# Two blocks on one core: the rows between the blocks are transposed from the sums, with both norms' gains joined in the column factor

## The chip, the cores and the metric

The kernel runs on one core of a Trainium2 chip. The metric is the device time of one execution in microseconds, the median of the runs shown. The engines are called as the profile calls them: PE (TensorE), ACT (ScalarE), DVE (VectorE), POOL (GpSimd) and SP, whose queue issues the weight loads.

## What is computed

The input is 256 rows of 1024 columns. A first block of two layers and a second block of two layers follow each other. Between them stand two norms in a row, one at the end of the first block and one at the start of the second:

```python
def rms_norm(x, g):
    xf = x.astype(jnp.float32)
    y = xf * lax.rsqrt(jnp.mean(xf * xf, axis=-1, keepdims=True) + EPS)
    return (y * g.astype(jnp.float32)).astype(x.dtype)

# first block, its end
    h2 = rms_norm(x, norm2_g[l])
    x = x + jnp.square(jax.nn.relu(h2 @ w_up[l])) @ w_down[l]
    return rms_norm(x, final_norm_g)
# second block, its start
    h = x
    xn = rmsnorm(h, norm_mix[0])
    h = h + hybrid_mixer(xn, w_in[0], ...)
```

So the normed rows of the first block are both the residual stream `h` of the second block and the input of its first norm. With `r1` the root of the sums' rows and `r2` that of the second norm, the first product of the second block reads `x * final_norm_g * norm_mix` per column, times `r1 * r2` per row.

## The kernel before

All weights are streamed through the core in pieces of 512 rows by 512 columns (1 MB). SP loads a piece; ACT casts it to a high part `WH` in two halves (L1608); DVE subtracts that from the piece and gets the low part `WL`, in two halves too (L2169); PE multiplies high by high, low by high and high by low (L744, L745, L746, or L730, L731, L736 where the activations have just been turned). There are three places for cut pieces, so a piece is cut two pieces ahead of its use, and its cut waits until PE is done with the piece three before.

The activations lie transposed in `XTH` and `XTL`. `half` makes one half of them, 512 columns of both row tiles, in two steps: PE transposes four blocks into a bank (L841), ACT writes the high part with the norm's gain as factor per column (L1619, L1620), DVE the low part (L2181). The norm's factor per row (`rs`) is left out here and comes in when a product is read out of PSUM.

Each engine's program is written by hand, and each engine takes its instructions in that order. A generator per engine walks the same list of pieces; small tasks are put in a list `side` and advance one step at each `tick`.

The place of the change is the seam between the blocks. The last down projection of the first block (`mlp1`, layer 1) adds its sums to the rows `X` in two column halves (`add_x`, L2347). The second block then starts with the product `vf` (260 columns, pieces of 4 blocks), then `qkb` (512 columns), and so on.

- DVE, `first_of_two` (L2452): waits for the gain `GB1`, spread over the partitions by a load at L560, multiplies the first column half of both row tiles by it into `XN` (`times_gain(0)`, L2449, 2 instructions), and makes the low part of half 0.
- PE transposes `XN`; its half 0 waits for `tg.at(0)` (L1071), half 1 for `tg.at(1)` (L1475).
- DVE, `two_norms` (L2456), called at the first step of `vf`: `times_gain(1)`, the low part of half 1, then the numbers of the norms. The second mean is taken of `XN` and scaled by `r1` twice (L2462, L2464); POOL makes both roots (L629, L630, each L610 and L612); DVE joins them to `rs` (L2466) and writes the normed rows back, `X = XN * r1` (L2468, 2 instructions).
- ACT, `two_norms` (L1840): the high part of half 1, then per row tile the squares of `X` and the squares of `XN` (L1844, L1845), and one signal `n2q` at the end.
- The first reader of `rs` is ACT's read-out of `vf` (L1869). The forget gate follows as a side task, `fox_gate`: DVE L2552 to L2559, a power on POOL (L633), a logarithm on ACT (L1873), DVE L2565, and then two small sums over rows on PE (L1092 to L1094), which stand in PE's order behind the first row tile of the second `qkb` piece.

Of the kernel before, what the change touches and what calls it, by code (L numbers as in the profile page):

```python
# [12 lines left out]
ALU = mybir.AluOpType  # L13
ACT = mybir.ActivationFunctionType
# [225 lines left out]
def program(nc, dr, cf, cb, ci, out):  # L240
    ctx = ExitStack()
    with ctx:
# [139 lines left out]
        for l in range(2):  # L382
            for key, ap, n in ((("n1", l), dr["norm1_g"], 8), (("n2", l), dr["norm2_g"], 8), (("nm", l), dr["norm_mix_2"], 8),
# [3 lines left out]
                if key != ("n1", 0):  # L387
                    k = sum(v[1] for v in rows.values())
                    rows[key] = (k, n)
                    gains_in.append((GR[k:k + n, :], ap[l].rearrange("(c p) -> c p", p=P)))  # L390
        NG = sum(v[1] for v in rows.values())
        rows[("n1", 0)] = (NG, 8)

# [83 lines left out]

        tg, n2q = sig("tg", 2), sig("n2q", 1)
        par_a, par_v = sig("par_a", [("lame", 0), ("rth", 0)]), sig("par_v", [("lama", 0), ("lamd", 0), ("rtl", 0)])
# [218 lines left out]
        def tensor():  # L698
# [327 lines left out]
            for l in range(2):  # L1026
# [40 lines left out]
                if l == 0:  # L1067
                    mlp1(l, lambda: half(("n1", 1), X, 0, (xadd.at("m1", 0, 0, 1), None)))
                else:
                    lane.side.append(iter(range(9)))  # L1070
                    mlp1(l, lambda: half(("nm", 0), XN, 0, (tg.at(0), None)))  # L1071

# [398 lines left out]
            for l in range(2):  # L1471
                for kp, t in group(("in2", l, "vf"), 260):
                    if (kp, t) == (0, 0):
                        if l == 0:
                            half(("nm", 0), XN, 1, (tg.at(1), None))  # L1475
                        else:
                            half(("nm", 1), X, 1, (xadd.at("pg", 0, 1, 1), None))
# [118 lines left out]
        def scalar():  # L1596
# [243 lines left out]
            def two_norms():  # L1840
                half(("nm", 0), 1, gain4(("nm", 0), 1))
                for t in range(T):
                    act.wait_ge(*xadd.at("m1", 1, 1, 1))
                    act.activation(NJ[2 * t], X[:, t, :], ACT.Square, scale=D ** -0.5, accum_out=ss[:, t:t + 1])  # L1844
                    m = act.activation(NJ[2 * t + 1], XN[:, t, :], ACT.Square, scale=D ** -0.5, accum_out=q2[:, t:t + 1])  # L1845
                m.then_inc(*n2q.inc(0))

            def qk_task(l, name, to, rot=False):
# [311 lines left out]
        def vector():  # L2160
# [27 lines left out]
            def gains():  # L2188
                dve.wait_ge(*gt.at(1))
                dve.tensor_copy(G[:, 0:NG], PS[:, 7, 0:NG]).then_inc(*gcol.inc(1))  # L2190
                yield
                dve.wait_ge(*gcol.at(1))
                dve.tensor_tensor(lt[:, 0:4], gc(("hb", 0), 0, 4), gc(("hb", 1), 0, 4), ALU.max).then_inc(*own.inc())
                dve.wait_ge(*own.now())
# [256 lines left out]

            def first_of_two():  # L2452
                dve.wait_ge(ld_f1, 16)
                times_gain(0)
                half(("nm", 0), 0, gain4(("nm", 0), 0))

            def two_norms():
                times_gain(1)
                half(("nm", 0), 1, gain4(("nm", 0), 1))
                dve.wait_ge(*n2q.at(0))  # L2460
                dve.wait_ge(*rsd.at("two", 0))
# [3 lines left out]
                dve.wait_ge(*rsd.at("two", 1))  # L2465
                dve.tensor_tensor(rs, r1, r2, ALU.mult).then_inc(*rs0.inc(0))  # L2466
                for t in range(T):
                    m = dve.tensor_scalar(X[:, t, :], XN[:, t, :], r1[:, t:t + 1], None, ALU.mult)  # L2468
                m.then_inc(*own.inc())

            for l in range(2):
# [57 lines left out]
                if l == 0:  # L2529
                    mlp1(l, lambda: half(("n1", 1), 0, gain4(("n1", 1), 0)))  # L2530
                else:
                    lane.side.append(second_params())
                    mlp1(l, first_of_two)

# [369 lines left out]
            for l in range(2):  # L2904
                for i, kp, t in lane.up(("in2", l, "vf")):
                    if (kp, t) == (0, 0):
                        if l == 0:
                            two_norms()
                        else:
                            half(("nm", 1), 1, gain4(("nm", 1), 1))  # L2910
                lane.side.append(fox_gate(l))
                lane.tick()
                lane.fine = True
# [184 lines left out]
```

## Time and profile before

| | us |
|---|---|
| median of 3 runs | 2435.8 |
| lowest and highest | 2435.73, 2435.89 |
| the profiled execution, its own time | 2439.0 |
| the profiled execution, its span | 2437.7 |
| PE busy in the span | 2398.9 (98%) |
| DVE busy | 1753.1 (72%) |
| ACT busy | 1492.1 (61%) |
| POOL busy | 79.9 (3%) |

All times of rows are counted from the start of the span. A row's duration runs to the end of the instruction, and the next instruction of the same engine may start a little before it, since instructions overlap in the pipeline: what an instruction costs its engine is the distance from its start to the next start. The idle time in brackets is that of the engine before the instruction, with what ended it.

### The profile page before, as it was taken

What the parts mean: (1) busy time and instruction counts of PE and PEld (TensorE: products, weight loads), DVE (VectorE), ACT (ScalarE), POOL (GpSimd) and SP (SyncE); (2) the same over time, 40 slices, a digit from 0 to 9 for tenths busy, and PEclk for the clock granted to TensorE, in tenths of its full rate; (3) what the DMA queues carried; (4) which work ended last, traced back from release to release, by engine and by line L of the source; (5) the groups of instructions that cost most, each with busy time, mean ns of one, the idle gap of its engine ahead of it and who ended that gap; (6) DMA issues with size and microseconds to landing.
All of it is one profiled execution on the core that took longest, in us unless ns stands there. A gap on an engine that the chain in (4) does not pass through costs nothing.

```text
span 2437.7 us, 30658 instructions
## 1 busy us (share of the span) xinstructions
PE 2398.9 (98%) x12208; PEld 2027.1 (83%) x12208; DVE 1753.1 (72%) x2127; ACT 1492.1 (61%) x1946; POOL 79.9 (3%) x105
## 2 busy tenths in 40 slices
PE   8999999999999998999999999999999999999998
PEld 7888899888888997888888878888888888888886
DVE  5655655566456555565555579999999999999996
ACT  5345544544554445554446667787777777777775
POOL 0000010000000000010000100000000000000000
PEclk9999999999999999999999999999999999999999
DMA  8453565554546554345555369999999999999992
GB/s 288 139 175 125 179 249 189 183 163 140 171 139 198 190 180 158 127 149 184 172 180 179 122 234 386 394 394 377 386 377 388 376 385 380 384 381 380 383 367 96
DMA packets 267952, 612.09 MB, mean 251 GB/s; under 512 B 12400, under 2 KB 17366, under 8 KB 267804
## 3 DMA queue, kind: packets, MB, share of 16 engines
q1 hardware_dynamic: 263324, 594.31, 68.8%
q0 software_dynamic: 4320, 15.49, 1.6%
q8 instruction: 99, 1.62, 0.3%
q14 instruction: 49, 0.40, 0.1%
q10 hardware_dynamic: 160, 0.27, 0.0%
HBM read 599.26 MB, written 11.01 MB: 250 GB/s over the span
## 4 chain that ended last, share of the span: by engine, by line
PE 95%; DVE 3%; ACT 1%; issue 0%; DMA 0%; POOL 0%; SPq 0%; DVEq 0%; ACTq 0%
PE PS L744 24%; PE PS L746 24%; PE PS L745 24%; PE PS L798 3%; PE PS L794 3%; PE PS L796 2%; PE PS L736 2%; PE PS L730 2%; PE PS L731 2%; PE PS L886 1%; PE PS L1333 1%; DVE WL L2169 1%; PE PS L841 1%; PE PS L850 1%; PE PS L956 1%; PE PS L925 1%
## 5 line engine op out<-in xcount | busy, mean ns | idle before, releaser
L2169 DVE TENSOR_TENSOR WL<-raw,WH 128x1024 fp32r<-128x1024 f32 (+2 forms) x796 | 930.3, 1210 | 305.3 <-ACT WH L1608 299.7
L1608 ACT CAST WH<-raw 128x1024 fp32r<-128x1024 f32 (+2 forms) x796 | 792.4, 1042 | 322.3 <-PE PS L746 277.0
L744 PE MATMUL PS<-WH,XTH 128*128 128x512 f32 (+2 forms) x1944 | 770.9, 397 | 0.0
L746 PE MATMUL PS<-WH,XTL 128*128 128x512 f32 (+2 forms) x1944 | 754.4, 388 | 0.0
L745 PE MATMUL PS<-WL,XTH 128*128 128x512 f32 (+2 forms) x1944 | 752.8, 387 | 0.0
L746 PEld LDWEIGHTS PS<-WH,XTL 128*128 128x128 f32 x1944 | 365.6, 188 | 76.5
L744 PEld LDWEIGHTS PS<-WH,XTH 128*128 128x128 f32 x1944 | 365.9, 188 | 72.7 <-issue 2.7
L745 PEld LDWEIGHTS PS<-WL,XTH 128*128 128x128 f32 x1944 | 366.3, 188 | 69.4
L2169 DVE TENSOR_TENSOR WL<-AR,WH 128x1024 fp32r<-128x1024 f32 x334 | 391.5, 1220 | 26.7 <-ACT WH L1608 26.0
L1608 ACT CAST WH<-AR 128x1024 fp32r<-128x1024 f32 x334 | 334.2, 1052 | 66.0 <-PE PS L746 65.9
L744 PE MATMUL PS<-WH,HTH 128*128 128x512 f32 x706 | 275.6, 390 | 2.9 <-issue 2.9
L746 PE MATMUL PS<-WH,HTL 128*128 128x512 f32 x706 | 275.4, 390 | 0.0
L745 PE MATMUL PS<-WL,HTH 128*128 128x512 f32 x706 | 275.3, 390 | 0.0
L744 PEld LDWEIGHTS PS<-WH,HTH 128*128 128x128 f32 x706 | 132.9, 188 | 31.1 <-issue 3.1
L745 PEld LDWEIGHTS PS<-WL,HTH 128*128 128x128 f32 x706 | 132.9, 188 | 27.6
L746 PEld LDWEIGHTS PS<-WH,HTL 128*128 128x128 f32 x706 | 132.8, 188 | 27.6
L794 PE MATMUL PS<-XTH,WH 128*128 128x256 f32 x512 | 143.9, 283 | 0.0
L798 PE MATMUL PS<-XTH,WL 128*128 128x256 f32 x512 | 143.8, 283 | 0.0
L796 PE MATMUL PS<-XTL,WH 128*128 128x256 f32 x480 | 135.8, 283 | 0.0
L794 PEld LDWEIGHTS PS<-XTH,WH 128*128 128x128 f32 x512 | 98.2, 192 | 0.7
L798 PEld LDWEIGHTS PS<-XTH,WL 128*128 128x128 f32 x512 | 98.2, 192 | 0.0
L796 PEld LDWEIGHTS PS<-XTL,WH 128*128 128x128 f32 x480 | 92.1, 192 | 0.5
(338 smaller groups left out, 1967.0 us busy)
## 6 DMA issues: line engine op xcount, KB each, us to landing
raw<-in_w_in SPq DMA_DIRECT2D x92, 1024.0 KB, 5.2
raw<-in_moe_w_gate SPq DMA_DIRECT2D x57, 1024.0 KB, 7.6
raw<-in_moe_w_up SPq DMA_DIRECT2D x57, 1024.0 KB, 8.0
AR<-in_moe_w_down SPq DMA_DIRECT2D x57, 1024.0 KB, 7.8
AR<-in_moe_w_gate SPq DMA_DIRECT2D x55, 1024.0 KB, 7.7
AR<-in_moe_w_up SPq DMA_DIRECT2D x55, 1024.0 KB, 8.1
raw<-in_moe_w_down SPq DMA_DIRECT2D x55, 1024.0 KB, 8.2
raw<-in_w_up SPq DMA_DIRECT2D x32, 1024.0 KB, 5.6
```

The lines of the kernel that those rows point to most:

```text
L730: pe.matmul(o, lh(2 * c + d), a[k + d], start=start and d == 0, stop=False, skip_group_check=True)
L731: pe.matmul(o, lh(2 * c + d), b[k + d], start=False, stop=False, skip_group_check=True)
L736: m = pe.matmul(o, ll(2 * c + d), a[k + d], start=False, stop=stop and d == 1, skip_group_check=True)
L744: pe.matmul(o, lh, rh, start=start, stop=False, skip_group_check=True)
L745: pe.matmul(o, lh, rl, start=False, stop=False, skip_group_check=True)
L746: return pe.matmul(o, ll, rh, start=False, stop=stop, skip_group_check=True)
L794: pe.matmul(o[s], a[k + d][:, cs[s]], h, start=start and s + d == 0, stop=False, skip_group_check=True)
L796: m = pe.matmul(o[s], a[k + d][:, cs[s]], XTL[:, 2 * c + d, :], start=False, stop=False, skip_group_check=True)
L798: m = pe.matmul(o[s], b[k + d][:, cs[s]], h, start=False, stop=stop and d == 1, skip_group_check=True)
L841: m = pe.transpose(PS[:, b0 + r, c * 256 + t * P:c * 256 + t * P + P], src[:, t, cc * P:cc * P + P], ident)
L1608: act.copy(WH[:, i % WR, c], slots[s][:, c]).then_inc(*wh.inc(i, h))
L2169: dve.tensor_tensor(WL[:, i % WR, c], slots[s][:, c], WH[:, i % WR, c].bitcast(F32), ALU.subtract).then_inc(*wl.inc(i, h))
```

## The change

Names and lines below are those of the kernel before, unless the text says otherwise.

- The final gain is loaded once more, as 8 rows of `GR` (one more small load on SP, and a transposition of 102 rows in place of 94). One more DVE instruction, in the side task `gains` in the first layer, multiplies the 8 columns of the gain `norm_mix` of layer 0 by it.
- PE transposes `X` at the seam, half 0 as soon as `xadd` of the first column half is there, half 1 with that of the second.
- DVE: `first_of_two` is gone. `two_norms` makes the low part of half 1 first, then both `times_gain`, 4 instructions in a row, then the numbers of the norms.
- ACT takes the squares of `X` for both tiles, signals, waits for `tg.at(1)`, and takes those of `XN` with a signal of their own.
- `X = XN * r1` leaves `two_norms` and becomes a side task, `rows_of_two`, behind the first step of `fox_gate`.

```diff
+        rows["gf"] = (NG, 8)
+        gains_in.append((GR[NG:NG + 8, :], dr["final_norm_g"].rearrange("(c p) -> c p", p=P)))
+        NG += 8
...
-                    mlp1(l, lambda: half(("nm", 0), XN, 0, (tg.at(0), None)))
+                    mlp1(l, lambda: half(("nm", 0), X, 0, (xadd.at("m1", 1, 0, 1), None)))
...
-                            half(("nm", 0), XN, 1, (tg.at(1), None))
+                            half(("nm", 0), X, 1, (xadd.at("m1", 1, 1, 1), None))
...
             def two_norms():
                 half(("nm", 0), 1, gain4(("nm", 0), 1))
+                act.wait_ge(*xadd.at("m1", 1, 1, 1))
                 for t in range(T):
-                    act.wait_ge(*xadd.at("m1", 1, 1, 1))
-                    act.activation(NJ[2 * t], X[:, t, :], ACT.Square, scale=D ** -0.5, accum_out=ss[:, t:t + 1])
-                    m = act.activation(NJ[2 * t + 1], XN[:, t, :], ACT.Square, scale=D ** -0.5, accum_out=q2[:, t:t + 1])
+                    m = act.activation(NJ[t], X[:, t, :], ACT.Square, scale=D ** -0.5, accum_out=ss[:, t:t + 1])
                 m.then_inc(*n2q.inc(0))
+                act.wait_ge(*tg.at(1))
+                for t in range(T):
+                    m = act.activation(NJ[2 + t], XN[:, t, :], ACT.Square, scale=D ** -0.5, accum_out=q2[:, t:t + 1])
+                m.then_inc(*n2q.inc(1))
...
+                dve.tensor_tensor(gc(("nm", 0), 0, 8), gc(("nm", 0), 0, 8), gc("gf", 0, 8), ALU.mult)
...
-            def first_of_two():
+            def two_norms():
+                half(("nm", 0), 1, gain4(("nm", 0), 1))
                 dve.wait_ge(ld_f1, 16)
                 times_gain(0)
-                half(("nm", 0), 0, gain4(("nm", 0), 0))
-
-            def two_norms():
                 times_gain(1)
-                half(("nm", 0), 1, gain4(("nm", 0), 1))
-                dve.wait_ge(*n2q.at(0))
+                dve.wait_ge(*n2q.at(1))
                 dve.wait_ge(*rsd.at("two", 0))
...
+            def rows_of_two():
+
                 for t in range(T):
                     m = dve.tensor_scalar(X[:, t, :], XN[:, t, :], r1[:, t:t + 1], None, ALU.mult)
                 m.then_inc(*own.inc())
+                yield
...
-                    mlp1(l, first_of_two)
+                    mlp1(l, lambda: half(("nm", 0), 0, gain4(("nm", 0), 0)))
...
                 lane.side.append(fox_gate(l))
+                if l == 0:
+                    lane.side.append(rows_of_two())
```

How the instructions stand on two engines. In the rows, `sm` is the tile of small numbers (means, roots, gate values), `AR` the work area that holds `GB1`, and an `x2` at the end is two instructions alike.

DVE, from the second `add_x` of the first block to the write-back of the rows, before (`X` is the last of the sums, `XN` the rows times the gain):

```order
L2347 SCALAR_TENSOR_TENSOR X<-PS,sm,X 128x512
L2169 TENSOR_TENSOR WL<-raw,WH 128x1024 [waits s_wh] x2
L2449 TENSOR_TENSOR XN<-X,AR 128x512 [waits s_xadd]
L2449 TENSOR_TENSOR XN<-X,AR 128x512
L2181 SCALAR_TENSOR_TENSOR XTL<-PS,G,XTH 128x256 [waits s_xh]
L2181 SCALAR_TENSOR_TENSOR XTL<-PS,G,XTH 128x256
L2181 SCALAR_TENSOR_TENSOR XTL<-PS,G,XTH 128x256 [waits s_xh]
L2181 SCALAR_TENSOR_TENSOR XTL<-PS,G,XTH 128x256
L2462 TENSOR_TENSOR sm<-sm 128x2 [waits s_rsd,s_n2q]
L2464 TENSOR_TENSOR sm<-sm 128x2 [waits v_step]
L2466 TENSOR_TENSOR sm<-sm 128x2 [waits s_rsd]
L2468 TENSOR_SCALAR X<-XN,sm 128x1024 x2
```

The same place now, up to the number `rs`:

```order
L2175 TENSOR_TENSOR WL<-raw,WH 128x1024 [waits s_wh] x2
L2187 SCALAR_TENSOR_TENSOR XTL<-PS,G,XTH 128x256 [waits s_xh]
L2187 SCALAR_TENSOR_TENSOR XTL<-PS,G,XTH 128x256
L2187 SCALAR_TENSOR_TENSOR XTL<-PS,G,XTH 128x256 [waits s_xh]
L2187 SCALAR_TENSOR_TENSOR XTL<-PS,G,XTH 128x256
L2457 TENSOR_TENSOR XN<-X,AR 128x512 [waits s_xadd,ld_f1]
L2457 TENSOR_TENSOR XN<-X,AR 128x512
L2457 TENSOR_TENSOR XN<-X,AR 128x512 [waits s_xadd]
L2457 TENSOR_TENSOR XN<-X,AR 128x512
L2467 TENSOR_TENSOR sm<-sm 128x2 [waits s_rsd,s_n2q]
L2469 TENSOR_TENSOR sm<-sm 128x2 [waits v_step]
L2471 TENSOR_TENSOR sm<-sm 128x2 [waits s_rsd]
```

The multiplications (L2449, now L2457) stood ahead of each low part; now all four stand behind the second one, and the write-back `X<-XN,sm` is not there any more.

DVE, from `rs` or the write-back to the last step of the gate before PE's row sums, before:

```order
L2468 TENSOR_SCALAR X<-XN,sm 128x1024 x2
L2169 TENSOR_TENSOR WL<-raw,WH 128x1024 [waits s_wh] x2
L2552 SCALAR_TENSOR_TENSOR sm<-PS,sm,BF 128x4 [waits s_e2,ld_m]
L2552 SCALAR_TENSOR_TENSOR sm<-PS,sm,BF 128x4 [waits s_e2]
L2555 TENSOR_SCALAR sm<-sm 128x8 [waits s_lfe]
L2557 TENSOR_TENSOR sm<-sm 128x8 [waits v_step]
L2559 TENSOR_SCALAR sm<-sm 128x8 [waits s_fz]
L2565 TENSOR_TENSOR sm<-sm 128x8 [waits s_fl,v_step]
L2169 TENSOR_TENSOR WL<-raw,WH 128x1024 [waits s_wh] x2
```

And now:

```order
L2471 TENSOR_TENSOR sm<-sm 128x2 [waits s_rsd]
L2175 TENSOR_TENSOR WL<-raw,WH 128x1024 [waits s_wh] x2
L2561 SCALAR_TENSOR_TENSOR sm<-PS,sm,BF 128x4 [waits s_e2,ld_m]
L2561 SCALAR_TENSOR_TENSOR sm<-PS,sm,BF 128x4 [waits s_e2]
L2564 TENSOR_SCALAR sm<-sm 128x8 [waits s_lfe]
L2566 TENSOR_TENSOR sm<-sm 128x8 [waits v_step]
L2568 TENSOR_SCALAR sm<-sm 128x8 [waits s_fz]
L2476 TENSOR_SCALAR X<-XN,sm 128x1024 [waits v_step]
L2476 TENSOR_SCALAR X<-XN,sm 128x1024
L2574 TENSOR_TENSOR sm<-sm 128x8 [waits s_fl,v_step]
L2175 TENSOR_TENSOR WL<-raw,WH 128x1024 [waits s_wh] x2
```

The write-back (L2468, now L2476) moved from ahead of the cut of the second `qkb` piece to behind the gate's first step; the gate's second step (L2565, now L2574) stands behind it.

ACT, from the last high part of the turn to the next cast of a weight piece, before:

```order
L1620 ACTIVATE XTH<-PS,G 128x256
L1844 ACTIVATE AR,sm<-X 128x1024 [waits s_xadd]
L1845 ACTIVATE AR,sm<-XN 128x1024
L1844 ACTIVATE AR,sm<-X 128x1024 [waits s_xadd]
L1845 ACTIVATE AR,sm<-XN 128x1024
L1608 CAST WH<-raw 128x1024 [waits s_wdone,ld_w1]
```

And now:

```order
L1623 ACTIVATE XTH<-PS,G 128x256
L1847 ACTIVATE AR,sm<-X 128x1024 [waits s_xadd]
L1847 ACTIVATE AR,sm<-X 128x1024
L1851 ACTIVATE AR,sm<-XN 128x1024 [waits s_tg]
L1851 ACTIVATE AR,sm<-XN 128x1024
L1611 CAST WH<-raw 128x1024 [waits s_wdone,ld_w1]
```

The two squares of `X` come first; those of `XN` wait for the multiplications.

## Rows read from the trace of the kernel before

**Rows 1.** Waits of PE, 930 to 975 us: who waited for whom, total, times, longest

```profile
PE PS L841 <- DVE XN L2449: 5.8, 2, 4.2
```

**Rows 2.** Timeline of DVE, 939 to 951 us: start, duration, line, operation [idle before]

```profile
939.97 1.41 DVE L2347 SCALAR_TENSOR_TENSOR X<-PS,sm,X 128x512 f32<-128x512 f32 x2 [0.77 <-PE PS L746]
941.48 1.29 DVE L2449 TENSOR_TENSOR XN<-X,AR 128x512 f32<-128x512 f32 x2
944.40 1.66 DVE L2181 SCALAR_TENSOR_TENSOR XTL<-PS,G,XTH 128x256 fp32r<-128x256 f32 x4 [1.62 <-ACT XTH L1620]
945.98 1.40 DVE L2347 SCALAR_TENSOR_TENSOR X<-PS,sm,X 128x512 f32<-128x512 f32 x2
947.29 2.35 DVE L2169 TENSOR_TENSOR WL<-raw,WH 128x1024 fp32r<-128x1024 f32 x2
949.56 1.29 DVE L2449 TENSOR_TENSOR XN<-X,AR 128x512 f32<-128x512 f32 x2
```

**Rows 3.** Timeline of PE, 942 to 967 us

```profile
942.83 1.09 PE L841 MATMUL PS<-CF,XN 128*128 128x128 f32 x8 [1.61 <-DVE XN L2449]
...
950.90 1.17 PE L841 MATMUL PS<-CF,XN 128*128 128x128 f32 x8 [4.17 <-DVE XN L2449]
...
956.23 0.28 PE L744 MATMUL PS<-WH,XTH 128*128 128x260 f32 x1
...
957.66 0.40 PE L744 MATMUL PS<-WH,XTH 128*128 128x512 f32 x1
...
963.11 0.39 PE L744 MATMUL PS<-WH,XTH 128*128 128x512 f32 x1
...
966.76 0.38 PE L1092 MATMUL PS<-sm,CF 128*128 128x4 f32 x2 [0.76 <-DVE sm L2565]
```

**Rows 4.** Timeline of ACT, 951 to 958 us

```profile
951.59 0.47 ACT L1619 ACTIVATE XTH<-PS,G 128x256 fp32r<-128x256 f32 x1 [4.19 <-PE PS L841]
...
953.03 1.07 ACT L1844 ACTIVATE AR<-X 128x1024 f32<-128x1024 f32 x1
...
957.19 2.00 ACT L1608 CAST WH<-raw 128x1024 fp32r<-128x1024 f32 x2
```

**Rows 5.** Timeline of DVE, 958 to 967 us

```profile
958.52 0.16 DVE L2462 TENSOR_TENSOR sm<-sm 128x2 f32<-128x2 f32 x1 [4.40 <-POOL sm L612]
...
960.10 1.41 DVE L2468 TENSOR_SCALAR X<-XN,sm 128x1024 f32<-128x1024 f32 x2
...
961.42 2.35 DVE L2169 TENSOR_TENSOR WL<-raw,WH 128x1024 fp32r<-128x1024 f32 x2
...
963.69 0.34 DVE L2552 SCALAR_TENSOR_TENSOR sm<-PS,sm,BF 128x4 f32<-128x4 f32 x2
...
966.53 0.17 DVE L2565 TENSOR_TENSOR sm<-sm 128x8 f32<-128x8 f32 x1 [1.88 <-ACT sm L1873]
```

**Rows 6.** Timeline of POOL, 964 us

```profile
964.52 1.64 POOL L633 TENSOR_TENSOR sm<-BASE,sm 128x8 f32<-128x8 f32 x1 [4.54 <-DVE sm L2557]
```

**Rows 7.** Waits of ACT over the whole run, the one row with a weight load

```profile
ACT WH L1608 <- DMA raw<-in_w_in: 1.4, 2, 0.7
```

**Rows 8.** Timeline of POOL, at 1042 and 2415 us

```profile
1042.53 1.03 POOL L612 TENSOR_TENSOR sm<-sm,HALF 128x4 f32<-128x4 f32 x1
...
2415.25 1.75 POOL L612 TENSOR_TENSOR sm<-sm,HALF 128x2 f32<-128x2 f32 x1
```

**Rows 9.** Timeline of DVE, at 1031 and 1042 us

```profile
1031.49 0.56 DVE L2632 TENSOR_TENSOR sm<-sm 128x1 f32<-128x1 f32 x1
...
1042.72 0.16 DVE L2632 TENSOR_TENSOR sm<-sm 128x1 f32<-128x1 f32 x1
```

**Rows 10.** Stretches: PE, PEld, DVE, ACT, POOL busy, clock, DMA share, GB/s

```profile
940.00:945.00 5.00, 3.39 (x20) 2.63 (x19) 3.27 (x6) 1.48 (x4) 0.00 (x0) 1.00 0.65 210
...
952.00:955.00 3.00, 3.00 (x16) 3.00 (x15) 1.66 (x4) 3.00 (x7) 0.00 (x0) 0.50 0.74 281
```

More of the change, by code:

```diff
@@ L475, in program @@
         mt, mth, mtl = sig("mt", [k for k in MLPR if k[0] == "m2"]), sig("mth", MLPR), sig("mtl", MLPR)
-        tg, n2q = sig("tg", 2), sig("n2q", 1)
+        tg, n2q = sig("tg", 2), sig("n2q", 2)
         par_a, par_v = sig("par_a", [("lame", 0), ("rth", 0)]), sig("par_v", [("lama", 0), ("lamd", 0), ("rtl", 0)])
```

## The prediction

> **What bounds the kernel now.** PE is busy for 98% of the span, so I looked first for who makes PE wait, then for the place of the change. In the waits of PE around the seam one row stands out: the transpositions wait 5.8 us in two waits for the multiplied rows [rows 1]. The timelines show why. In the first wait (1.61 us) PE's sums are added on DVE from 939.97 for 1.41 us, then multiplied from 941.48 for 1.29 us, and only then PE starts, at 942.83 [rows 2, 3]. In the second (4.17 us) DVE adds at 945.98, cuts a weight piece at 947.29, multiplies at 949.56, and PE starts at 950.90 [rows 2, 3]. After that wait the granted clock is 0.50, the lower of the two levels (1.2 GHz), in the stretch 952 to 955 us [rows 10]. Later in the seam PE waits once more, 0.76 us, for the forget gate, at 966.76 [rows 3]. This last point is where the sum has to be taken: what PE wins earlier counts only as far as the gate's chain comes earlier too.
>
> **The change, part by part.** All times are on the clock of the profiled span.
>
> *First half.* The multiplications leave the path. PE followed their end (941.48 + 1.29 = 942.77) by 0.06. Behind the end of the sums (939.97 + 1.41 = 941.38) it can start at 941.44, and it is free then (942.83 - 1.61 = 941.22) [rows 2, 3]. That is 1.39 earlier, and all that hangs on it moves along: the low parts from 944.40 to 943.01, the second sums from 945.98 to 944.59, their end to 946.00 [rows 2].
>
> *Second half.* PE starts 0.06 behind these sums, at 946.05, where it was 950.90: 4.85 earlier, because the multiplications (2 x 0.6) and the piece that stood ahead of them (949.56 - 947.29 = 2.27) are gone from ahead of the transpositions [rows 2, 3]. PE has then waited about 0.7 us in place of 4.17.
>
> *DVE behind it.* The piece is cut from 945.90 (sums + 1.31), the low parts of half 1 start at 948.17 (+ 2.27) and take 1.58 (945.98 - 944.40) [rows 2]. They wait for nothing else: ACT's first high part follows PE by 0.69 (951.59 - 950.90) and both of that step are done by about 947.6 [rows 3, 4]. So the four multiplications run from 949.75. Two take 1.29; four, at 0.605 from start to start, end at 952.25.
>
> *ACT.* Its high parts end where the squares begin, 2.13 behind PE (953.03 - 950.90), at 948.2. Four squares took 4.16 (957.19 - 953.03), so two take 2.08 [rows 3, 4]. Those of `X` are done at 950.3. Those of `XN` wait for 952.3 and their sums are there 2.1 + 0.2 later (the reading of the last sum lies behind the square), at 954.6. POOL takes the first root beside that, from 950.3. It has room: even where DVE works without a pause on two SBUF inputs, its power took 1.75 [rows 8], and it has 4.3.
>
> *The numbers.* From DVE's L2462 to the end of `rs` 1.58 passed (960.10 - 958.52), POOL's second root within it [rows 5]. So `rs` is there at 956.2. The write-back of the rows, which cost 961.42 - 960.10 = 1.32, has left this place [rows 5]. The cut of the second `qkb` piece starts at 956.2, the gate at 958.45 (963.69 - 961.42 = 2.27), and PE's row sums follow the gate's start by 966.76 - 963.69 = 3.07, at 961.5 [rows 3, 5]. Before it was 966.76: **5.2 us earlier**.
>
> *Is PE itself there by then?* From 946.05: transpositions 0.85; 12 short matmuls at full clock 1.43 (957.66 - 956.23) to 948.3; 4 high ones, then a wait for the low parts until about 949.05 and again near 949.9; the second row tile ends at 951.55. The first `qkb` piece takes 5.45 (963.11 - 957.66) to 957.0 [rows 3]. There PE waits some 0.4 for the first half of the next low part (956.2 + 1.2), does 12 matmuls (2.72) and is ready at 960.1. So PE waits about 1.4 us for the gate, where it was 0.76. The short clock loss is gone, but it lay in front of this wait and is worth nothing beyond it. Nothing that follows differs from before, and all of it starts from this point, so the 5.2 stay.
>
> *What is added.* One small load on SP, about 0.3 us of its queue, before the sixth weight piece; in the whole run ACT waited for weights 1.4 us in two waits, both before that [rows 7], so zero. One small DVE product in a layer where DVE is busy a good half of the time: zero, between 0 and 0.2. POOL's first root now falls into the multiplications. DVE and POOL do hold each other up: a DVE product of single numbers took 0.56 in place of 0.16 while POOL read large tiles [rows 9]. Two short POOL operations that read two numbers each can hold the multiplications by 0.1, bounds 0 and 0.4. I take 0.1.
>
> *The write-back in its new place* is the cost that the trace of before does not show. It takes 1.32 on DVE, from 959.45 to 960.8. DVE's next step on the chain is due at 961.3 (966.53 - 966.76 before PE), so it has 0.5 to spare if it can start at once. But POOL begins the gate's power at 959.3, and this takes 1.64 [rows 6]. Lower bound, no hold: 0. Upper bound, the write-back waits for the end of the power at 960.93 and the gate's step follows at 962.3: 1.0. The nearest row is a DVE product on two inputs that ran at its usual 0.16 at 1042.72, 0.2 us into a power that POOL had begun at 1042.53 [rows 8, 9]. I take 0 and keep 1.0 as a rival.
>
> *Sum.* -5.2 + 0.1 = -5.1 us. On the profiled execution (2439.0, its span 2437.7) this gives 2433.9. The median of the runs shown is 3.2 lower, 2435.8, and the seam is made of the same instructions there, so: 2435.8 - 5.1 = **2430.7 us**.
>
> **The rivals.**
>
> *A, the write-back is held by POOL.* The write-back has one large input and one large output and takes 0.66 us for 1024 columns (half of 1.32), where a cut with two inputs takes 1.14 (half of 2.27) [rows 2, 5]: it moves twice as much per cycle, so it may need what POOL uses for writing also, and the row at 1042.72 is no evidence for such an instruction. Then the gate's second step comes 1.0 later: 2435.8 - 4.1 = 2431.7 us. The Trainium skill ("SBUF — State Buffer", the section on SBUF's two separate sides) says that a DVE operation in a two-port mode and a GpSimd operation exclude each other for the whole instruction, whoever starts first. By that rule POOL, which starts first, wins. For reads by two inputs this trace doesn't bear "whole instruction" out (0.16 at 1042.72 inside a power of 1.03), for the two-port form no row shows anything. 40 in 100.
>
> *B, the gain is lost or half lost further on*, because the weight loads set the pace of the expert stage: 2435.8 down to 2433, middle 2434. Against it: ACT waited for no load there [rows 7], and loads are started by DVE's cuts, which come earlier as well. 4 in 100.
>
> *C, the chain is shorter than added up*, by up to 1.4, since PE is ready at 960.1: 2429.3. It would need the latencies between five engines' steps to be shorter than in the rows. 5 in 100.
>
> *D, slower: the clock.* The seam now has four short waits of PE in a row (0.7, 0.2, 0.4, 1.4) in place of one long. If they brought the clock to the lower level from 947 on and it stayed there, each matmul would stand twice as far from the next: the 36 short ones 0.12 more (1.43 / 12), the long ones 0.23 more (5.45 / 24) [rows 3]. The long ones up to the end of the second `qkb` piece are 48: 4.3 + 11.0 = 15.3. Less the 1.8 that PE waits anyway, that is 13.5, and 2435.8 - 5.1 + 13.5 = 2444.2. It turns the sign once the lower level lasts for about 11 of the long ones (5.1 + 1.8 = 4.3 + 11 x 0.23). Against it: the wait of 1.61 was followed by a stretch at 1.00, only the one of 4.17 by 0.50 [rows 3, 10]. 1 in 100.
>
> **How the numbers follow.** My forecast has 50 in 100, with a range of its own of 2430.2 to 2431.2: some ten links between engines, each known to 0.05 or so, and the 0.4 of POOL's hold. A difference of 0.2% is 4.87 us here, about what a measurement of this kernel can tell from no change, so the line lies at 2430.93. In my forecast four fifths fall below it (40), the rest within. A falls within, but for a tenth of it (4). C is faster (5), B within, D slower. Faster: 0.40 + 0.04 + 0.05 = 0.49, less 0.03 for what I haven't thought of: 0.46. Of these, 0.01 goes to slower, which is 0.02 with D, and 0.02 to within: 0.10 + 0.36 + 0.04 + 0.02 = 0.52. The range to hold the time 8 times in 10 takes in the forecast and A with half a microsecond around them: 2429.8 to 2432.4.
>
> **What would show it.** In the profile of the changed kernel the two waits of the transpositions (5.8) shrink to about 0.9 in all, and the granted clock stays at 1.00 through the seam. The four multiplications run in a row some 2 us behind the low parts' start, and ACT waits about 2 us for them between its squares. PE waits about 0.4 for a low part at the second `qkb` piece and 1.4 for the gate, whose row sums come near 961.5. The write-back shows rival A by its duration: 0.75 if it is free, over 2 us with POOL's power ending first if it is held, and then the row sums come near 962.5. I would be wrong altogether if the distance from the row sums to the end of the span were other than before (2437.7 - 966.8 = 1470.9), or if the start of the kernel had a wait for a load that wasn't there.

## The result

The changed kernel takes **2431.0 us** (median of 18 runs, 2429.8 to 2432.9 but for one run at 2978 whose granted clock was 0.757), the kernel before 2436.6 us beside it (18 runs, 2435.7 to 2438.3). The ratio is 0.9976, with a 95% interval of 0.9970 to 0.9983: 0.24% faster, 5.6 us. Two further sessions gave 2430.8 and 2430.6 against 2437.0 and 2437.1, ratio 0.9974 (0.9963 to 0.9984) both times. So the gain is 5.6 to 6.5 us, where 5.1 were forecast. That the forecast's 2430.7 is met within 0.3 us is in part luck: the three runs it started from (2435.8) lay 0.8 us below the median of more runs, and the gain was forecast too small by 0.5 or more.

### The profile page after: what moved, and what is told of

Read it like the earlier page. It is cut to its first block, busy times and chain, and to the rows that moved or that the text cites. A ratio compares the mean times of both kernels' runs of the same rounds, so it can differ in the third digit from the quotient of the medians.

```text
span 2428.8 us, 30660 instructions
## 1 busy us (share of the span) xinstructions
PE 2396.3 (99%) x12208; PEld 2026.0 (83%) x12208; DVE 1753.1 (72%) x2128; ACT 1492.2 (61%) x1946; POOL 82.2 (3%) x105
## 3 DMA queue, kind: packets, MB, share of 16 engines
q8 instruction: 99, 1.62, 0.3%
## 4 chain that ended last, share of the span: by engine, by line
PE 96%; DVE 3%; ACT 1%; issue 0%; DMA 0%; POOL 0%; SPq 0%; DVEq 0%; ACTq 0%
PE PS L747 24%; PE PS L749 24%; PE PS L748 24%; PE PS L801 3%; PE PS L797 3%; PE PS L799 2%; PE PS L739 2%; PE PS L733 2%; PE PS L734 2%; PE PS L889 1%; PE PS L1336 1%; PE PS L844 1%; DVE WL L2175 1%; PE PS L853 1%; PE PS L959 1%; PE PS L928 1%
## 5 line engine op out<-in xcount | busy, mean ns | idle before, releaser
L2175 DVE TENSOR_TENSOR WL<-raw,WH 128x1024 fp32r<-128x1024 f32 (+2 forms) x796 | 930.6, 1211 | 306.0 <-ACT WH L1611 299.3
L1611 ACT CAST WH<-raw 128x1024 fp32r<-128x1024 f32 (+2 forms) x796 | 792.5, 1042 | 322.0 <-PE PS L749 276.9
L2175 DVE TENSOR_TENSOR WL<-AR,WH 128x1024 fp32r<-128x1024 f32 x334 | 391.7, 1222 | 26.6 <-ACT WH L1611 25.8
```

The source lines that it names most:

```text
L1611: act.copy(WH[:, i % WR, c], slots[s][:, c]).then_inc(*wh.inc(i, h))
L2175: dve.tensor_tensor(WL[:, i % WR, c], slots[s][:, c], WH[:, i % WR, c].bitcast(F32), ALU.subtract).then_inc(*wl.inc(i, h))
```

## The profile after

Line numbers of the changed kernel are a few higher: L2355 adds the sums, L2175 cuts a piece, L2187 makes the low part, L2457 multiplies by the gain, L2476 writes the rows back, L2574 is the last step of the gate on DVE, L1095 its row sums on PE, L844 the transpositions, L636 the gate's power on POOL.

| profiled execution | before | after |
|---|---|---|
| its own time, us | 2439.0 | 2430.1 |
| span, us | 2437.7 | 2428.8 |
| PE busy | 2398.9 (98%) | 2396.3 (99%) |
| DVE busy | 1753.1 (72%) | 1753.1 (72%) |
| ACT busy | 1492.1 (61%) | 1492.2 (61%) |
| POOL busy | 79.9 (3%) | 82.2 (3%) |

The two spans differ by 8.9 us, the medians by 5.6. Some 3 of the 8.9 aren't the change's, as the experiments show; so I read the seam by itself, as one distance: from the start of the first sums on DVE to the gate's row sums on PE. Before it is 966.76 - 939.97 = 26.79 [rows 2, 3].

Waits of PE, 930 to 975 us, of the changed kernel (who waited for whom, total, times, longest); it answers to [rows 1]:

```profile
PE PS L1095 <- DVE sm L2574: 1.0, 1, 1.0
PE PS L844 <- DVE X L2355: 0.9, 2, 0.7
```

The transpositions wait 0.9 us in all, for the sums instead of the multiplied rows, where they waited 5.8. The timeline of PE in the same stretch, to be laid beside [rows 3]:

```profile
941.21 1.09 PE L844 MATMUL PS<-CF,X 128*128 128x128 f32 x8 [0.21 <-DVE X L2355]
...
945.81 1.09 PE L844 MATMUL PS<-CF,X 128*128 128x128 f32 x8 [0.69 <-DVE X L2355]
...
957.10 0.50 PE L747 MATMUL PS<-WH,XTH 128*128 128x512 f32 x1
...
961.13 0.39 PE L1095 MATMUL PS<-sm,CF 128*128 128x4 f32 x2 [1.01 <-DVE sm L2574]
```

The second transpositions stand 4.60 behind the first (8.07 before), and the distance of the seam is 961.13 - 939.74 = **21.39**: 5.40 less. Timeline of DVE, for [rows 2, 5]:

```profile
939.74 1.41 DVE L2355 SCALAR_TENSOR_TENSOR X<-PS,sm,X 128x512 f32<-128x512 f32 x2 [0.76 <-PE PS L749]
942.77 1.66 DVE L2187 SCALAR_TENSOR_TENSOR XTL<-PS,G,XTH 128x256 fp32r<-128x256 f32 x4 [1.62 <-ACT XTH L1623]
944.35 1.40 DVE L2355 SCALAR_TENSOR_TENSOR X<-PS,sm,X 128x512 f32<-128x512 f32 x2
945.67 2.35 DVE L2175 TENSOR_TENSOR WL<-raw,WH 128x1024 fp32r<-128x1024 f32 x2
947.93 1.66 DVE L2187 SCALAR_TENSOR_TENSOR XTL<-PS,G,XTH 128x256 fp32r<-128x256 f32 x4
949.50 2.50 DVE L2457 TENSOR_TENSOR XN<-X,AR 128x512 f32<-128x512 f32 x4
954.25 0.16 DVE L2467 TENSOR_TENSOR sm<-sm 128x2 f32<-128x2 f32 x1 [2.26 <-ACT AR L1851]
...
955.83 2.35 DVE L2175 TENSOR_TENSOR WL<-raw,WH 128x1024 fp32r<-128x1024 f32 x2
...
959.09 1.42 DVE L2476 TENSOR_SCALAR X<-XN,sm 128x1024 f32<-128x1024 f32 x2
960.91 0.17 DVE L2574 TENSOR_TENSOR sm<-sm 128x8 f32<-128x8 f32 x1 [0.40 <-ACT sm L1879]
```

The multiplications stand fourth now, behind all that PE needs. The write-back at 959.09 fills time in which DVE idled before: 1.88 us idle ahead of the gate's last step [rows 5], 0.40 now. Timeline of POOL, for [rows 6]:

```profile
950.23 1.86 POOL L613 TENSOR_SCALAR sm<-sm 128x2 f32<-128x2 f32 x1 [179.97 <-ACT AR L1847]
952.17 0.71 POOL L615 TENSOR_TENSOR sm<-sm,HALF 128x2 f32<-128x2 f32 x1
...
958.93 1.64 POOL L636 TENSOR_TENSOR sm<-BASE,sm 128x8 f32<-128x8 f32 x1 [3.21 <-DVE sm L2566]
```

The gate's power takes 1.64, as before, with the write-back beside it. The clock, in stretches of the changed kernel (PE, PEld, DVE, ACT, POOL busy, clock, DMA share, GB/s), for [rows 10]:

```profile
948.00:950.00 2.00, 1.96 (x16) 1.74 (x16) 2.00 (x6) 2.00 (x5) 0.00 (x0) 1.00 0.41 59
950.00:952.00 2.00, 2.00 (x17) 1.92 (x16) 2.00 (x4) 0.14 (x2) 1.77 (x1) 1.00 1.02 383
952.00:955.00 3.00, 3.00 (x15) 2.48 (x14) 0.32 (x2) 2.97 (x5) 1.02 (x3) 1.00 0.18 63
```

It stays at 1.00 (2.4 GHz); before it was 0.50 from 952 to 955.

## The experiments

In the table "seam" is the distance defined above, "late stretch" the one from the start of POOL's last indirect load to the start of the statistics of the end (before: 2413.53 - 2344.44). Each ratio is taken against runs of the kernel before on the same chip in the same session, whose medians were 2436.6 to 2437.1.

| kernel | seam, us | late stretch, us | median, us | ratio to before |
|---|---|---|---|---|
| before | 26.79 | 69.1 | 2436.6 | 1 |
| before_again | 26.81 | 66.0 | (one run) 2436.3 | |
| load_only | 27.39 | 66.1 | 2437.1 | 1.0000 (0.9990 to 1.0010) |
| rows_only | 26.75 | 66.0 | 2435.8 | 0.9995 (0.9985 to 1.0004) |
| keep_wait | 26.16 | 66.1 | 2436.3 | 0.9998 (0.9989 to 1.0007) |
| undo_rows | 22.75 | 66.1 | 2432.0 | 0.9983 (0.9974 to 0.9992) |
| rows_twice | 22.47 | 68.6 | 2432.9 | 0.9982 (0.9972 to 0.9992) |
| after | 21.39 | 66.1 | 2431.0 | 0.9976 (0.9970 to 0.9983) |
| after_again | 21.40 | 66.1 | 2430.8 | 0.9974 (0.9963 to 0.9984) |
| after_third | 21.38 | 66.4 | 2430.6 | 0.9974 (0.9963 to 0.9984) |
| gain_early | 20.18 | 66.3 | 2429.9 | 0.9973 (0.9963 to 0.9983) |
| gain_early_again | 20.17 | 65.9 | 2429.7 | 0.9969 (0.9957 to 0.9981) |

**1. The wait put back (keep_wait).** The changed kernel, with the four multiplications ahead of the low part of half 1, and PE's half 1 waiting for them. The data, the loads and the place of the write-back are those of the change.

```diff
-                            half(("nm", 0), X, 1, (xadd.at("m1", 1, 1, 1), None))
+                            half(("nm", 0), X, 1, (tg.at(1), None))
...
-                half(("nm", 0), 1, gain4(("nm", 0), 1))
                 dve.wait_ge(ld_f1, 16)
                 times_gain(0)
                 times_gain(1)
+                half(("nm", 0), 1, gain4(("nm", 0), 1))
```

> The changed kernel, but all four multiplications stand ahead of the low part of half 1 and PE's second transpositions wait for them, as before; the first half comes straight from the sums. Theory: PE starts the second half 10.75 us after the first sums (before: 10.93, changed: 6.07), its wait is near 4.9 us, the granted clock falls to 0.50 for some 3 us behind it, and PE is at the row sums only at a distance of 25.9: 0.9 of the 5.4 us are left. Rival (the order of norms and write-back brings most of it, not the second half's wait): distance 24.1, the clock low or not. The time is 4.5 (theory) or 2.7 (rival) above the changed kernel.

Measured: seam 26.16, 4.77 longer than with the change; median 5.3 us above the changed kernel's of the first session (5.4 by the two ratios to before). Its waits of PE, 930 to 975 us, two stretches, and PE's second transpositions and row sums:

```profile
PE PS L844 <- DVE XN L2457: 5.4, 1, 5.4
...
948.00:950.00 2.00, 0.00 (x0) 0.00 (x0) 2.00 (x5) 0.00 (x0) 0.00 (x0) 0.55 0.29 35
...
952.00:955.00 3.00, 3.00 (x15) 3.00 (x15) 1.73 (x4) 2.99 (x7) 0.00 (x0) 0.50 0.24 88
...
950.66 1.97 PE L844 MATMUL PS<-CF,X 128*128 128x128 f32 x8 [5.37 <-DVE XN L2457]
...
966.08 0.28 PE L1095 MATMUL PS<-sm,CF 128*128 128x4 f32 x2
```

This one order undoes nearly the whole gain. PE doesn't wait for the gate here at all: with the long wait and the low clock behind it, PE itself is the last to come. The 4.77 can be split by the rows. The second transpositions start 10.74 behind the first sums (939.92) instead of 6.07: 4.67 later. From there PE needs 15.42 to the row sums instead of 14.31, its wait left out: 1.11 more, in a stretch that ran in part at the lower clock. Against that goes the wait of 1.01 for the gate, which the changed kernel has and this one hasn't. What the first half alone is worth wasn't tried.

**2. The write-back, moved back and moved alone.** undo_rows is the changed kernel without the side task, with the write-back in `two_norms` again; rows_only is the kernel before with nothing but this move.

```diff
                 dve.tensor_tensor(rs, r1, r2, ALU.mult).then_inc(*rs0.inc(0))
-
-            def rows_of_two():
-
                 for t in range(T):
                     m = dve.tensor_scalar(X[:, t, :], XN[:, t, :], r1[:, t:t + 1], None, ALU.mult)
                 m.then_inc(*own.inc())
-                yield
...
-                if l == 0:
-                    lane.side.append(rows_of_two())
```

> The changed kernel with the write-back of the rows (X = XN * r1, two DVE instructions) back in its old place, ahead of the cut of the second qkb piece. Measure: the distance from the start of the first sums on DVE to PE's row sums of the gate, 26.79 us before (939.97 to 966.76) and 21.39 in the changed kernel (939.74 to 961.13). Theory (the serial chain of DVE, ACT and POOL sets the row sums): the full 1.32 us comes back, distance 22.7, time the changed kernel's plus 1.3. Rival (PE sets the point and the chain has room): PE waits 1.0 us there, so it would cost 0.3 at most, distance 21.7.

> The kernel before with one part of the change alone: the write-back moved behind the gate's first step; the transpositions still wait for the multiplied rows. Theory: the chain gets 1.32 us shorter, but PE waits only 0.76 us for it before, so PE becomes the bound and 0.75 us are won: distance 26.0, time 0.7 to 0.8 below the kernel before. Rival (the parts simply add up): 1.3 us, distance 25.5. Rival (POOL's power holds the write-back once it stands there): nothing is won, 26.5 to 26.8.

undo_rows: 22.75, so the move is worth 1.36 in the changed kernel (the prediction put it at 1.32). Between the medians, of two sessions, lies 1.0, with ratios to before whose intervals overlap. rows_only: 26.75, not the 26.0 of the theory but a number that I had set down for a write-back that is held. Its rows say something else (timelines of DVE, POOL and PE):

```profile
964.49 1.42 DVE L2471 TENSOR_SCALAR X<-XN,sm 128x1024 f32<-128x1024 f32 x2
966.30 0.17 DVE L2569 TENSOR_TENSOR sm<-sm 128x8 f32<-128x8 f32 x1 [0.40 <-ACT sm L1873]
...
964.32 1.64 POOL L633 TENSOR_TENSOR sm<-BASE,sm 128x8 f32<-128x8 f32 x1 [3.22 <-DVE sm L2561]
...
967.02 0.39 PE L746 MATMUL PS<-WH,XTL 128*128 128x512 f32 x1
967.25 0.28 PE L1092 MATMUL PS<-sm,CF 128*128 128x4 f32 x2
```

Nothing is held: the power takes 1.64, the write-back 1.42. The gate is ready at 966.30, 25.80 behind the first sums, but PE comes to its row sums at 967.25 with no wait. Read in stretches of 1 us, the clock was at 0.50 from about 949.8 to 956.7 in this profile, in the first one of before only from about 951.8 to 955.2. So the move alone is capped by PE. Beside load_only (27.39, see 4), whose clock fell as early, rows_only is 0.64 shorter, near the 0.75 that was expected; its median is 1.0 below that of before in its session, but the interval (0.9985 to 1.0004) reaches to no gain.

Added to the kernel before, the move gives 0.04 and the rest of the change, the transpositions from the sums above all, gives 4.04 (26.79 - 22.75, undo_rows), 4.08 in all. Taken out of the changed kernel, the move costs 1.36 and the order of the second half 4.77. Both together gave 5.40. So a part of the gain, 1.3 by the first count (0.7 if the 0.64 stands for the move), is had only with both parts: the shorter chain of DVE counts for something only where PE is ready before it.

**3. The write-back done twice (rows_twice).**

```diff
-                for t in range(T):
-                    m = dve.tensor_scalar(X[:, t, :], XN[:, t, :], r1[:, t:t + 1], None, ALU.mult)
-                m.then_inc(*own.inc())
+                for _ in range(2):
+                    for t in range(T):
+                        m = dve.tensor_scalar(X[:, t, :], XN[:, t, :], r1[:, t:t + 1], None, ALU.mult)
+                    m.then_inc(*own.inc())
+                    dve.wait_ge(*own.now())
```

> The changed kernel with VectorE's write-back of the rows done twice behind the gate's short instructions, with a wait for the first one between; outputs are the same. Theory, the write-back only uses idle time of VectorE while GpSimd raises the power and isn't slowed by it: the gate's last product waits only for VectorE now; it moves from 960.91 to about 962.0 (0.40 of idle time is eaten first), so the distance to the row sums is 21.39 + 1.1 = 22.5 and the time 1.0 to 1.1 more than the changed kernel; GpSimd's power stays at 1.64 us and each pair of write-backs at 1.42. Rival, VectorE and GpSimd hold one another: the power is stretched by the second pair to 2.8 us or more and the exponential of the gate goes after it, distance 23 or more, or a pair of write-backs takes over 1.5 us.

Seam 22.47, 1.08 more; the theory's 22.5. DVE, POOL and PE:

```profile
959.19 2.87 DVE L2477 TENSOR_SCALAR X<-XN,sm 128x1024 f32<-128x1024 f32 x4
...
959.03 1.64 POOL L636 TENSOR_TENSOR sm<-BASE,sm 128x8 f32<-128x8 f32 x1 [3.21 <-DVE sm L2568]
...
962.31 0.39 PE L1095 MATMUL PS<-sm,CF 128*128 128x4 f32 x2 [2.10 <-DVE sm L2576]
```

Four write-backs take 2.87, twice the 1.42 of two, and POOL's power, with write-backs beside it from its 0.16th us to its end, keeps its 1.64, as it does in undo_rows with no write-back beside it. Neither engine holds the other here. The median is 2.1 above that of the changed kernel in the same session. 1.1 of that is the seam; for the rest I have no row but the stall that its profile shows far behind the seam (6, below).

**4. Only what the change adds at the start (load_only).** The kernel before, with the eight rows of weights loaded and turned, and the product that nothing reads.

```diff
+        rows["gf"] = (NG, 8)
+        gains_in.append((GR[NG:NG + 8, :], dr["final_norm_g"].rearrange("(c p) -> c p", p=P)))
+        NG += 8
...
+                dve.tensor_tensor(gc("gf", 0, 8), gc(("nm", 0), 0, 8), gc("gf", 0, 8), ALU.mult)
```

> The kernel before with only what the change adds at the start of the program: the eight further rows of weights loaded, turned into columns, and the product with the first norm's weights, which nothing reads. Theory, both are covered: the first sums of the seam start at the same time as before (939.97 in its profile, 0.5 either way by the waits for loads at the start), distance 26.8, and the time is that of before within 0.2 per cent, most likely within 0.5 us. Rival, the fuller load and the extra product delay TensorE's start: the wait of TensorE for the first columns grows, everything behind it shifts by 0.3 us or more, and some of the change's gain was lost to it.

The time is that of before: ratio 1.0000. The start of the first sums was 940.72 in its profile, 0.75 later than in before's, as the rival had it. But the start of the seam moves by itself: over the three profiles without the load it is 939.80 to 940.50, over the nine with it 939.27 to 940.72, mean 940.1 and 939.9. So the load costs nothing that can be seen.

What I had not looked for stands in the seam. It is 27.39 here (940.72 to 968.11), 0.6 longer than in the two profiles of before, with the same instructions. Stretches of load_only, then of before_again:

```profile
948.00:950.00 2.00, 0.00 (x0) 0.00 (x0) 2.00 (x3) 0.16 (x1) 0.00 (x0) 0.99 0.00 0
950.00:952.00 2.00, 0.34 (x2) 0.35 (x3) 1.60 (x3) 0.00 (x0) 0.00 (x0) 0.50 0.28 31
952.00:955.00 3.00, 3.00 (x16) 3.00 (x15) 1.32 (x4) 2.18 (x5) 0.00 (x0) 0.50 0.88 329
955.00:957.00 2.00, 2.00 (x12) 2.00 (x12) 0.41 (x2) 2.00 (x5) 0.00 (x0) 0.55 0.03 8
```

```profile
948.00:950.00 2.00, 0.00 (x0) 0.00 (x0) 2.00 (x4) 0.00 (x0) 0.00 (x0) 1.00 0.00 0
950.00:952.00 2.00, 1.26 (x10) 1.27 (x11) 0.68 (x2) 0.57 (x2) 0.00 (x0) 0.90 0.63 131
952.00:955.00 3.00, 3.00 (x16) 3.00 (x16) 1.66 (x4) 3.00 (x8) 0.00 (x0) 0.50 0.70 268
955.00:957.00 2.00, 2.00 (x18) 2.00 (x18) 0.00 (x0) 2.00 (x5) 0.00 (x0) 0.99 0.02 4
```

After the same 4.17 us wait the clock is low already when PE starts again in the one, and falls only after that in the other. The eight transpositions, which the rest of the chain follows, take 1.97 us in place of 1.17:

```profile
951.65 1.97 PE L844 MATMUL PS<-CF,XN 128*128 128x128 f32 x8 [4.17 <-DVE XN L2453]
```

```profile
950.74 1.17 PE L841 MATMUL PS<-CF,XN 128*128 128x128 f32 x8 [4.17 <-DVE XN L2449]
```

Whether the early fall belongs to an execution or to a kernel is not shown: both profiles of before fell late, and the early ones (load_only, rows_only and, behind a wait of 5.37, keep_wait) are of other kernels. That the medians of load_only and before agree within 0.1 us speaks against a fixed 0.6 between these two.

**5. One multiplication pair back in an idle place (gain_early).** In the changed kernel ACT waits 1.89 us for the multiplications (the squares of `XN`), and DVE idles 1.62 us before the low part of half 0. gain_early does `times_gain(0)` in that gap; PE still turns the sums.

```diff
+            def first_of_two():
+                dve.wait_ge(ld_f1, 16)
+                times_gain(0)
+                half(("nm", 0), 0, gain4(("nm", 0), 0))
+
             def two_norms():
                 half(("nm", 0), 1, gain4(("nm", 0), 1))
-                dve.wait_ge(ld_f1, 16)
-                times_gain(0)
                 times_gain(1)
...
-                    mlp1(l, lambda: half(("nm", 0), 0, gain4(("nm", 0), 0)))
+                    mlp1(l, first_of_two)
```

> The changed kernel with the first two multiplications moved forward, to between the first sums and the low part of half 0, where DVE waits 1.62 us for ACT anyway; only two are left behind the low part of half 1. Theory: they need 1.29 us and fit in, so PE's first wait stays at 0.2; the chain to the gate gets 1.2 us shorter and then PE, which is ready 1.0 to 1.2 us before the row sums, is the bound: distance 20.2, time 1.2 us below the changed kernel. Rival (they push the low part of half 0, and the sums behind it): 0.1 to 0.3 us less early at the second half and a distance of 20.4 to 20.6. Rival (the chain's end is set elsewhere): no difference, 21.4.

> The kernel gain_early again, to set its median beside the changed kernel's in one session. If the 1.21 us by which its row sums came earlier (20.18 against 21.39) reach the end, its median is 1.2 below that of after_third, near 2429.8; the rival, that they are lost to a later wait, gives a difference under 0.4.

Timeline of DVE and the waits of PE (930 to 975 us) of gain_early:

```profile
940.98 1.29 DVE L2457 TENSOR_TENSOR XN<-X,AR 128x512 f32<-128x512 f32 x2
942.50 1.66 DVE L2187 SCALAR_TENSOR_TENSOR XTL<-PS,G,XTH 128x256 fp32r<-128x256 f32 x4 [0.22 <-ACT XTH L1623]
...
949.23 1.29 DVE L2457 TENSOR_TENSOR XN<-X,AR 128x512 f32<-128x512 f32 x2
...
PE PS L844 <- DVE X L2355: 0.9, 2, 0.7
PE PS L1095 <- DVE sm L2577: 0.2, 1, 0.2
```

Seam 20.18, 1.21 less, as expected, and PE's wait for the gate down to 0.2. The median in one session was 2429.7 against 2430.6 of the changed kernel (6 and 8 runs); before that it was 2429.9 against 2431.0, in two different sessions. The difference of 0.9 to 1.2 agrees with the seam; the ratios to before overlap in their intervals, so it rests on the traces and two pairs of medians. It is the fastest version of the study.

**6. The same kernels again (after_again, before_again, after_third).** Unaltered.

> The changed kernel once more, unaltered. All theories: from the start of the first sums to the row sums of the gate 21.4 us (21.39 in its first profile), clock 1.00 through the seam, no wait of TensorE over 0.8 us before the row sums. That the changed kernel owes part of its lead to a stall late in the program, which the profile of before had (2.9 us of issue near 2390 us) and that of the change had not: if the change removes it, it is absent here and present in before_again. If it varies from one execution to the next, as I hold (three kernels that share before's or the change's code had 1.4 us there), the stretch from the start of the indirect load at 2338.6 to the statistics at 2404.7 is 66.1 us in most profiles of either kernel.

> The kernel before once more, unaltered. The late stretch: 66 us if the stall varies by itself, 69.1 if it belongs to this kernel. The seam: the clock fell to 0.50 at about 951.9 in the first profile of before, but at 949.9 with the write-back moved alone, after the same stop of TensorE. If the moment of the fall varies by itself, it will lie anywhere from 1 us before to 2 us after the restart of TensorE at 950.9, and the distance from the first sums to the row sums is 26.8 where the low stretch is short (3.2 us) and up to 27 where it is long (6.5 us), since TensorE had 0.76 us to spare. If the moving of the write-back made the clock fall early, this run shows the short one again. The rival that the time after depends on this phase wants over 27.

> The changed kernel again, on the same chip as gain_early_again and in turn with it: distance from the first sums to the gate's row sums 21.4, median near 2431.0.

The seam repeats to 0.02 (after_again had 21.40). The late stretch of before_again is 66.0, so the 69.1 of the first profile weren't that kernel's. Nor are they bound to the kernel before: rows_twice, made from the changed one, has 68.6. The seam of before_again is 26.81 with the clock falling late; the expectation's rival, over 27 where it falls early, is what load_only showed. The waits of PE from 2340 to 2415 us, of before, of the changed kernel and of rows_twice:

```profile
PE PS L744 <- issue: 2.9, 1, 2.9
```

```profile
PE PS L747 <- DVE HTL L2829: 1.4, 1, 1.4
```

```profile
PE PS L747 <- issue: 2.5, 1, 2.5
```

Ten of the twelve profiles have a wait of 1.4 (once 1.8) for DVE at this place, these two a stall of 2.5 and 2.9 "issue". In rows_twice the clock is 0.51 behind it, from 2392 to 2395. In the late stretch that makes some 3 us between two profiles. What sets the stall off stays open.

## Why the prediction was right, and where it was off

Times of the prediction are compared on the clock of before's span; the seam began 0.23 earlier in the profile of after, so 0.23 is added to its rows.

- **Both halves on PE.** Predicted 941.44 and 946.05, measured 941.44 and 946.04. keep_wait shows that this is the cause: the order behind which PE's second half stands is worth 4.77 of the seam.
- **DVE behind it.** The cut was to start at 945.90, the low parts at 948.17, the multiplications at 949.75 and to end at 952.25. Measured: 945.90, 948.16, 949.73, 952.23.
- **The hold between POOL and the multiplications** was charged at 0.1 on DVE. It fell the other way round: the products took 2.50 and weren't held, POOL's first step was, 1.86 in place of 0.23. It was free, since ACT waited for the products anyway; even with it POOL's root was done at about 952.9, before the 954.25 at which it was wanted.
- **The numbers.** The sums of the squares were used at 954.48 (forecast 954.6), the second cut began at 956.06 (956.2), the gate at 958.33 (958.45), the row sums stood at 961.36 (961.5). The latency between engines was rounded up: 0.14 in all.
- **PE's own readiness.** PE was free at 961.13 - 1.01 + 0.23 = 960.35 (forecast 960.1) and waited 1.0 for the gate (forecast 1.4). The second row tile of `vf` ended 0.1 later than forecast (951.42 + 0.23 = 951.65, where 951.55 was set down). The order of who comes last was right, and the write-back's place matters for this reason alone: it moves DVE, and DVE leads the gate.
- **Rival A, the write-back held by POOL,** is refuted by the rows of the changed kernel and by rows_twice, for this pair: a power with 8 numbers a partition on POOL, a product of one large input by a number on DVE. The rule that the rival leaned on, exclusion for the whole instruction (the Trainium skill, "SBUF — State Buffer"), isn't borne out in any of the eight profiles with the write-back in its new place. (That the write-back uses two ports was argued from its 0.66 for 1024 columns; no run shows it.) For a DVE product of two inputs in SBUF against a POOL operation that reads SBUF the same section says the same, and there the traces agree in part. POOL's first step ended 0.09 us behind DVE's products (952.09 and 952.00); but it had begun at 950.23, in the second of four products (949.50, 950.10, 950.70, 951.30), so it was held through the next two as well and not for one instruction. The other way round, a DVE product of single numbers inside a POOL power wasn't held at all (0.16 at 1042.72, [rows 8, 9]).
- **Rival B, a gain lost in the expert stage,** didn't come. From the row sums to POOL's next instruction (L641, after the change L644) it is 63.98 before (1030.74 - 966.76) and 63.80 after (1024.93 - 961.13). From there to the memset ahead of the last indirect loads, through the whole expert stage, it is 1309.18 (2339.92 - 1030.74) and 1309.16 (2334.09 - 1024.93).
- **Rival C, a shorter chain,** named a floor that is real: PE's own readiness. gain_early reaches it but for 0.2 us, by moving instructions rather than by shorter latencies.
- **Rival D, the clock,** didn't come: 1.00 through the seam in all three profiles of the changed kernel.
- **The sign of being wrong altogether.** The distance from the row sums to the end of the span was to stay at 1470.9. It was 1467.7 (2428.8 - 961.1) in the profile of the changed kernel. But before_again has 1468.4 (2435.0 - 966.6), so most of the 3 us is the stall of the first profile (6, above) and not a failure of the sum.
- **The chances.** A gain of over 0.2% had been given 46 in 100 and one within it 52. It came out at 0.24%, the less likely of the two, for the reasons of the next two points.
- **What was undersized.** The sum said 5.1. The seam gave 5.40: 0.14 from latencies, 0.1 from the hold that wasn't, and a last 0.06 by which the first estimate was rounded down (5.26 to 5.2). The medians gave 5.6 to 6.5. The step that fell short is "The short clock loss ... lay in front of this wait and is worth nothing beyond it". It holds where the clock falls late, as it did in the profile I read. Where it falls early, as in load_only, the transpositions themselves run at the lower level, the chain gets 0.6 longer (27.39), and the change would take that off too: 6.0. I had one profile and took its moment of the fall as given. That the kernel before itself falls early in some executions wasn't seen (its two profiles fell late), so that this explains the rest between 5.4 and the medians is possible and not shown; the late stall, seen in a profile of before and in one of rows_twice, may blur medians by as much.
- **The base.** This error worked against the last one, and the two nearly cancelled: the three runs shown lay low, at 2435.8, where 13 to 31 runs in a session have their median at 2436.6 to 2437.1.

## What to carry to other kernels

Ask of each instruction on the path whether its result is needed by the next engine or only later: a factor per column that can be joined to another factor lets the next stage read the unscaled data, and the product itself can move behind it, or better into a gap in front (gain_early). Price a move of several parts against one end point that all paths meet in, with the readiness of each engine beside it; the parts added one at a time gave 0.0 and 4.0, taken out one at a time 1.4 and 4.8, and together 5.4. And before a difference between two profiles is explained, take a second profile of each: here a third of it was a stall that comes and goes.

## What the runs showed of the hardware

- After one and the same wait of PE of 4.17 us the granted clock fell at different moments: after the restart in both profiles of before (low from about 951.8 to 955.2 and from 951.6 to 955.0), before it in load_only and rows_only (from 950.0 to 956.8 and from 949.8 to 956.7). No kernel was seen with both, so whether the moment varies between executions is open. In this seam the early fall went with 0.6 us more between load_only and before. Waits of up to 1.01 us in the changed seam didn't lower it, nor did the 1.61 of before [rows 3, 10] or the 2.10 of rows_twice (1.00 from 960 to 965 us).
- DVE's products of two large inputs held a short POOL instruction until they were done. The timeline of POOL in gain_early, where the pair of products ends at 950.52, and in keep_wait, where DVE was idle:

```profile
949.96 0.65 POOL L613 TENSOR_SCALAR sm<-sm 128x2 f32<-128x2 f32 x1 [179.97 <-ACT AR L1847]
```

```profile
955.66 0.23 POOL L613 TENSOR_SCALAR sm<-sm 128x2 f32<-128x2 f32 x1 [185.22 <-ACT AR L1847]
```

  With four products it was 1.86, ending at 952.09, behind products that ended at 952.00; it got no turn between one product and the next. DVE's write-back, with one large input, neither slowed a POOL power that had begun 0.16 us before it nor waited for its end (1.64 and 1.42 with both at work).
- In two of twelve profiles PE paused 2.5 to 2.9 us near 2390 us for nothing that the profile shows, with the lower clock level behind it (0.51 from 2392 to 2395 in rows_twice, 0.60 from 2395 to 2398 in before). In the other ten a wait of 1.4 to 1.8 for DVE stands at this place.
